# A four-mixer block reordered: fourth mixer first, input, conditioning and gate tiles beside its chain and beside attention

## Time and profile before

| | us |
|---|---|
| median of 3 runs | 2001.17 (2000.5 to 2010.23) |
| the profiled execution | 2002.8 |
| its span, first to last instruction | 2001.0 |
| mean matmul of the norm behind `out` (L711) starts at | 487.7 |
| TensorE busy, share of the span | 1791.4, 90% |
| VectorE busy | 955.8, 48% |
| ScalarE busy | 748.4, 37% |

### The profile page before, as it was taken

How to read it: one execution, slowest core, us unless ns; L and a number is a source line. 1 busy time by engine, 2 the same in 40 slices (tenths; PEclk the granted TensorE clock), 3 DMA queues, 4 the chain that set the end, 5 groups by cost and what they waited for, 6 DMA issues and landing times.

```text
span 2001.0 us, 33267 instructions
## 1 busy us (share of the span) xinstructions
PE 1791.4 (90%) x12858; PEld 1364.6 (68%) x12858; DVE 955.8 (48%) x1744; ACT 748.4 (37%) x1370; POOL 111.9 (6%) x170
## 2 busy tenths in 40 slices
PE   7987685997799999799999899999998799989997
PEld 7934344997544444377778588788875685779997
DVE  3552635665712211326444555434534454458684
ACT  4433212443222112242464443333325334555454
POOL 0200000004100000100000200000002000010000
PEclk9989796999799999989999899999998899989998
DMA  6887292556198899722100222322221230135552
GB/s 245 172 324 267 104 345 77 175 185 205 39 335 324 330 339 338 290 87 74 53 1 22 74 85 85 95 95 95 88 91 64 84 106 1 43 116 189 180 179 75
DMA packets 84994, 303.95 MB, mean 152 GB/s; under 512 B 10160, under 2 KB 12208, under 8 KB 84720
## 3 DMA queue, kind: packets, MB, share of 16 engines
q1 hardware_dynamic: 80784, 291.02, 42.2%
q0 software_dynamic: 2736, 7.35, 1.6%
q10 hardware_dynamic: 1328, 3.55, 0.4%
HBM read 347.74 MB, written 3.15 MB: 175 GB/s over the span
## 4 chain that ended last, share of the span: by engine, by line
PE 74%; DMA 12%; DVE 8%; ACT 4%; issue 2%; SPq 1%; POOL 0%; DVEq 0%; ACTq 0%; POOLq 0%
PE bank L766 49%; PE bank L711 16%; DMA ring<-wall 11%; PE bank L1193 3%; PE bank L790 2%; PE bank L1231 1%; PE bank L1206 1%; PE bank L1216 1%; ACT BIG L1481 1%; DVE w_lo L1823 1%; DVE BIG L2383 1%; ACT w_hi L1421 0%; ACT L1483 0%; ACT XC L1489 0%; PE bank L1253 0%
## 5 line engine op out<-in xcount | busy, mean ns | idle before, releaser
L766 PE MATMUL bank<-BIG_f32r,w_hi 128*128 128x256 f32 (+1 forms) x2208 | 554.0, 339 | 26.7 <-DVE BIG_f32r L1836 17.0
L1823 DVE TENSOR_TENSOR w_lo<-ring,w_hi 128x1024 fp32r<-128x1024 f32 x261 | 325.3, 1256 | 296.7 <-ACT w_hi L1421 295.5
L766 PEld LDWEIGHTS bank<-BIG_f32r,w_hi 128*128 128x128 f32 x2208 | 382.8, 192 | 75.7 <-issue 27.9
L766 PE MATMUL bank<-BIG_f32r,w_lo 128*128 128x256 f32 (+1 forms) x1136 | 385.8, 340 | 0.0
L1421 ACT ACTIVATE w_hi<-ring 128x1024 fp32r<-128x1024 f32 x261 | 272.5, 1053 | 223.6 <-PE bank L766 212.0
L766 PE MATMUL bank<-AR_f32r,w_hi 128*128 128x256 f32 (+1 forms) x1066 | 267.9, 330 | 16.7 <-issue 9.4
L766 PEld LDWEIGHTS bank<-BIG_f32r,w_lo 128*128 128x128 f32 x1136 | 216.8, 191 | 26.2 <-issue 0.2
L766 PEld LDWEIGHTS bank<-AR_f32r,w_hi 128*128 128x128 f32 x1066 | 185.2, 192 | 37.5 <-issue 9.9
L766 PE MATMUL bank<-AR_f32r,w_lo 128*128 128x256 f32 (+1 forms) x448 | 147.7, 330 | 0.0
L766 PE MATMUL bank<-XC_f32r,w_lo 128*128 128x256 f32 x424 | 122.4, 289 | 0.0
L766 PE MATMUL bank<-XC_f32r,w_hi 128*128 128x256 f32 x424 | 121.8, 287 | 0.0
(11 more groups left out here) (361 smaller groups left out, 2313.5 us busy)
## 6 DMA issues: line engine op xcount, KB each, us to landing
ring<-wall SPq DMA_DIRECT2D x547, 512.0 KB, 4.5
w_extra<-wall SPq DMA_DIRECT2D x96, 512.0 KB
BIG<-t_rows POOLq DMA_DIRECT2D x16, 128.0 KB, 14.4
AR<-na_rows POOLq DMA_DIRECT2D x32, 64.0 KB, 7.2
con<-consts ACTq DMA_DIRECT2D x1, 1810.0 KB, 12.2
na_rows<-rpb_pad POOLq DMA_DIRECT2D x1, 1792.0 KB, 34.8
XC<-xin ACTq DMA_DIRECT2D x1, 1024.0 KB, 6.4
XC<-ctxin POOLq DMA_DIRECT2D x1, 1024.0 KB, 6.1
```

Source lines behind the costliest of these rows:

```text
L766: ins = nc.tensor.matmul(o, l, r, start=start and n == 0, stop=stop and n == 2, **kw)
L1823: V.tensor_tensor(w_lo[:, i % SPLIT_RING, :], ring[:, t % RING, :], w_hi[:, i % SPLIT_RING, :].bitcast(F32), ALU.subtract).then_inc(w_spli ...
```

## The change

Nothing is computed otherwise, but in another order and in other places.

- The stream is no longer laid out stage by stage. A table `BESIDE` names the points of the program at which input tiles, gate tiles and pairs are worked off, and the stream follows it. Split and whole tiles now alternate, so `feed` looks ahead over the whole tiles in between, as far as the ring (six) and three split tiles reach.
- Order: the low-rank inputs and mixer d's inputs (7 tiles), d's features, its families and chunks, with the other 18 input tiles and 21 pairs beside them; then index scores, d's norm, attention with 23 gate tiles and 16 pairs, of which the choice of keys now takes two rounds in each of the first four steps; then mixer c with 9 gate tiles and 9 pairs; then eight branch tiles and eight out tiles in turns.
- Gates are copied out of PSUM as they come, all kept (8 x 1024 columns), and pass the sigmoid later, 1024 columns at once.
- `iw` has no tile of its own any more (8 columns inside `small`, transposed by a matmul): 169 tiles in place of 170.
- `out` is summed over k outermost into four banks that are all finished at the end; before, one result after another was finished.
- d's shift is done for each of the seven inputs as it arrives, where one 128 x 1792 and seven 128 x 256 operations were done at once.
- The 29 modulation operations run inside the expert loop, behind expert 2.

```diff
+BESIDE = {
+    "lora": ins_("small", "dr0", "dr1", "dk0"),
+    "kk": ins_("dk1", "dv0", "dv1"),
+    "feat": ins_("iq0", "iq1", "ik", "ckv") + ada_(2),
+    "split": ins_("bq0", "bq1") + ada_(2),
+    "Z1": ins_("cq") + ada_(1),
+    "D4": ada_(1),
+    "Z2": ins_("ck") + ada_(1),
+    "Z3": ins_("cv0"),
+    "Pm": ins_("cg0") + ada_(1),
+    "P2t": ins_("cg1", "aq0"),
+    "Y1": ins_("aq1") + ada_(1),
+    "T": ins_("ak0"),
+    "chain": ins_("ak1", "av0"),
+}
+for _c in range(NCH):
+    for _w in ("X", "U", "Yc"):
+        BESIDE[f"{_w}{_c}"] = ada_(1)
+BESIDE["var"] = gates_(7, 0, 1)
+BESIDE["std"] = ada_(2) + gates_(7, 2, 3)
+for _t in range(8):
+    BESIDE[f"att{_t}"] = ada_(2 if _t < 5 else 1) + gates_(6 - _t // 2, 2 * (_t % 2), 2 * (_t % 2) + 1)
+for _t in range(8, 11):
+    BESIDE[f"att{_t}"] = ada_(1) + gates_(2, _t - 8)
+BESIDE["c0"] = gates_(2, 3) + ada_(1)
+BESIDE["c1"] = gates_(1, 0, 1) + ada_(2)
+BESIDE["c2"] = gates_(1, 2) + ada_(1)
+BESIDE["c3"] = gates_(1, 3) + ada_(1)
+BESIDE["c4"] = gates_(0, 0, 1) + ada_(2)
+BESIDE["c5"] = gates_(0, 2, 3) + ada_(2)
...
+    def split_until(t):
+
+        if t >= moe0:
+            return split_at[min(t + SPLIT_RING, run_end(t + 1)) - 1] + 1
+        end = split_at[t]
+        while end < split_at[t] + SPLIT_RING and split_order[end] < min(t + RING, moe0):
+            end += 1
+        return end
...
+            for m in range(KC + 1):
+                if m < KC:
+                    for half in range(2):
+                        b = open_(("br", m, half))
+                        w = tile("branch", m)
...
+                if m:
+                    k = m - 1
+                    pe.wait_ge(sem("merged_split"), k + 1)
+                    w = tile("out", k)
+                    for o in range(KC):
+                        split_product(out_banks[o // 2][:, (o % 2) * S:(o % 2 + 1) * S], w, o, mg_hi[:, k, :],
...
+                    if st == "att1":
+                        beside(f"att{t}")
+                        if t < 4:
+                            choose(2 * t)
+                            choose(2 * t + 1)
+                        if t == 3:
+                            select()
...
+            in_unit("small")
+            in_unit("dr0")
+            in_unit("dr1")
+            act.wait_ge(sem("d_shifted"), 1)
...
+            dve.wait_ge(sem("params_in"), 16)
+            dve.wait_ge(sem("consts_in"), 16)
+            shifted(0)
...
+                if n == 2:
+                    modulation()
```

More of the change, by code:

```diff
@@ new lines, with early_stream @@
+BESIDE["c4"] = gates_(0, 0, 1) + ada_(2)
+BESIDE["c5"] = gates_(0, 2, 3) + ada_(2)
+R_W, R_A, R_G, R_C = 0, 32, 64, 96
+def early_stream():
+    items, pair = [], 0
+    for work in BESIDE.values():
+        for w in work:
+            if w[0] == "in":
+                items += [("in", IN_BLOCKS.index(n)) for n in (w[1], IN_PAIRS.get(w[1])) if n]
+            elif w[0] == "gate":
+                items.append(("gate", 4 * w[1] + w[2]))
+            else:
+                items += [("ada", 2 * pair), ("ada", 2 * pair + 1)]
+                pair += 1
+    for m in range(KC + 1):
+        if m < KC:
+            items.append(("branch", m))
+        if m:
+            items.append(("out", m - 1))
+    return items
@@ L1067, in _ @@
             family("Kt", pair(tok(DD["Kh"]), eye))
+            b = open_("bonus")
+            pe.wait_ge(sem("d_bonus_in"), 1)
+            mm(b, c_("blockones"), bn.rearrange("p a b -> p (a b)"), done="bonus")
+            beside("split")
             pe.wait_ge(sem("d_split"), 5)
@@ new lines, in _ @@
+            b = open_("ymean")
+            for c in range(NCH):
+                for p in range(2):
+                    evacuated(pe, ("Yc", c, p))
+            mm(b, c_("blockones"), yT.rearrange("p a b -> p (a b)"), done="ymean")
+            beside("var")
+            b = open_("yvar")
+            pe.wait_ge(sem("d_ysq"), 1)
+            mm(b, c_("blockones"), DD["t"].rearrange("p a b -> p (a b)"), done="yvar")
+            index_scores(1)
+            beside("std")
+            pe.wait_ge(sem("bias1"), 16 * 16)
@@ L1644, in _ @@
[L1644 to L1652 removed]
+            beside("c4")
@@ L1659, in _ @@
-            act.wait_ge(sem("merged"), KC)
-            tell(f(mg_hi[:, KC - 1, :], mergedT[:, KC - 1, :], ACT.Copy), "merged_high")
-            for m in range(KC):
-                feed("out", m)
+                    if m < KC:
+                        feed("branch", m)
+                    feed("out", m - 1)
             layer_norm("a")
@@ L2043, in _, with beside @@
-            step(ins, "ys_ready")
-            r_, k_, v_ = dS[:, 1:3, :], dS[:, 3:5, :], dS[:, 5:7, :]
-            evacuated(dve, "dw")
-            evacuated(dve, "da")
-            evacuated(dve, "dg")
-            for m in range(2):
-                ins = V.tensor_scalar(DD["kk"][:, m, :], k_[:, m, :], p_("d_k_k")[:, m:m + 1], None, ALU.mult)
-            step(ins, "d_kk")
+                    feed_to(k + 1)
+            def beside(point):
+                for work_ in BESIDE[point]:
+                    if work_[0] == "in":
+                        feed_in(work_[1])
+                    elif work_[0] == "gate":
+                        feed("gate", 4 * work_[1] + work_[2])
@@ L2110, in _ @@
                     evacuated(dve, (fam, p))
+            beside("chain")
             for c in range(NCH):
@@ L2162, in _ @@
+            step(V.reciprocal(c_sq, c_sq))
+            step(V.tensor_tensor(c_o, c_o, c_sq, ALU.mult))
+            for m in range(2):
+                ins = V.scalar_tensor_tensor(ysT[:, 2, m, :], c_o[:, m, :], p_("c_norm_gain")[:, m:m + 1],
+                                             F["cg"][:, m, :], ALU.mult, ALU.mult)
+            step(ins, "c_out")
+            ys_low(3, 3)
+            beside("c5")
+            ys_low(2, 4)
             b = bank(dve, "mods")
```

933 lines of the change are left out of this document (516 added, 417 removed).

## The result

Measured together, the changed kernel took 1980.57 us (median of 4, 1976.11 to 1985.88), the kernel before 2003.71 (median of 4): ratio 0.988, 95% interval 0.985 to 0.991. It is faster by 23 us. I forecast 1939 us, a saving of 64: right in direction, but 42 us too optimistic, with a saving little more than a third of the forecast's. The time lies inside the wide range (1893 to 1988) and outside the forecast's own (1915 to 1965).

What follows compares the result with a forecast made beforehand. Waiting left by the hand-written order was taken to decide, not TensorE's floor (348 us) or the ring's (254). Eight steps summed to 424.0 against 487.7, saving 63.7, hence 1939 us; own range 1915 to 1965, 8 in 10 from 1893 to 1988.

Steps and rivals of the forecast that it cites:

- step 1: From the start to d's features: 62.8 us, with eleven blocks of 32.6 us and three waits on top.
- the price of choice: Choice of keys inside attention's first four steps: 1.6 us a step, plus 2 us for the selected bias, 8.4 us.
- step 8: First norm: GpSimd's adds no longer run beside blocks, last add to mean matmul costs 4.5 us more, to 424.0.
- step 2: d's families and blocks: 79.7 us, to 142.5; 18.2 to the first squaring, then 61.5.
- step 3: Four chunks with twelve pairs beside them: 32 us, to 174.5; the pairs' 6 us lie in TensorE's gaps.
- step 4: Index scores and d's norm: 30 us, to 204.5, with four gate blocks of 11.5 and two waits.
- step 5: Attention: 109 us, to 313.5; the loop takes 25.6 us for two steps, with a gate tile landing behind four tiles.
- step 6: Mixer c: 50 us, to 363.5; nine gates 25.8, nine pairs 4.5, c's own 8, waits about 9.
- Steps 7 and 8: Branch and out in turns, 56 us at 6.1 for each of eight, then the norm's added 4.5, to 424.0.
- A: Rival, whole new order: the waits vanish as engines run ahead, 48 us less, 1891 us; chance 0.16.
- B: Rival, at 25 wait points: the clock falls, 1.55 us extra each, 39 us in all, 1978 us; chance 0.17.
- C: Rival, VectorE's queue: conversions waiting for tiles block it, 3.5 us at 25 points, 87 us, 2026 us; chance 0.09.

Runs made afterwards that it cites:

- e6: Changed kernel with all eight rounds of choice and the selected bias ahead of attention again, on VectorE; 1987.51 us.
- e8: Changed kernel with the first norm's sum made by seven TensorE matmuls instead of six GpSimd adds, seven VectorE routing operations moved behind the norm; 1977.09 us.
- e9: Changed kernel with the sixteen bias1 transfers held until the mean of d's result is read and na_rows until the merge; 1992.04 us.
- e1: Changed kernel with the one transfer na_rows issued right after the constants landed, instead of behind the bias1 transfers; 1978.89 us.
- e4: Changed kernel with conversions ahead ending at the next whole tile, from the gate tiles of d's norm to the branch; 2003.72 us.
- e5: Changed kernel with conversions ahead ending at the next whole tile, from d's norm's gate tiles only to gate (2, 1) of attention's tenth step; 1983.05 us.
- e11: Changed kernel with late bias1 and na_rows, the first norm's mean on TensorE, and pair and gate alternating in attention only; 1971.13 us.
- e15: Changed kernel with five of attention's pairs moved among the later families; 1971.64 us.
- e16: Changed kernel with five of attention's pairs among the later families, na_rows early and the norm's mean on TensorE; 1957.95 us, ratio to before 0.977.
- e3: Changed kernel with pair and gate tiles alternating in attention and in places of mixer c; 1973.25 us.
- e7: Changed kernel with the sigmoid taken when a gate is copied out of its bank, instead of later; 1981.62 us.
- e2: e1 with the bias rows t5 also computed ahead of the chain, so the sixteen bias1 transfers are issued earlier; 1987.82 us.
- e12: Changed kernel with five of attention's thirteen pairs moved in front of the features; 1975.1 us.
- e13: Changed kernel with eight pairs moved in front of the features, five left in attention; 1974.89 us.
- e14: e12 with na_rows early and the first norm's mean on TensorE; 1968.19 us.

## Why the prediction was right and wrong

**What held.** Blocks beside the chains keep the clock up and save time; step 1 (62.1 for 62.8); the price of choice (e6, 7.0 us for 8.4); step 8's adds (e8); the loop of branch and out, bound by TensorE, 265 matmuls in 32.05 us.

**The step that failed** is "Four pairs took 1.92 us, so 0.5 us a pair on TensorE". It is a term of the sum that was mis-sized: 0.96 us, and 0.26 for the picking, which the sum left out. Over 48 pairs that is 0.74 x 48 = 35 us of TensorE work, in a sum that came out 35.6 us too small. That the two numbers agree is chance. By the stages below the pairs can account for 20 us at most: 2.9 in step 2, 3.3 in step 3, 1.5 in step 4, 5.9 in step 5 and 6.7 in step 6. The largest miss, 16.2 us in step 2, is mostly other work that the sum priced too low. What fell on the path is seen stage by stage:

- *Step 2*, 61.5 us forecast from the first squaring on. In e9, where the transfers are away, the 71.1 us are 36.8 for twelve blocks (3.07 each between small work, 2.90 in the long run of blocks; forecast 34.4), 29.4 for everything else on TensorE (forecast 19.8), and 4.9 in which it was idle (forecast 7.3). In the 29.4, families took 1.04 to 1.08 us each and not 0.86, a price that the forecast gave without a row: 3 us more. Matmuls at the low clock were some 4 us, pairs and picking 2.9 (the forecast took six pairs, the table has five there), the rest small. The waits that I worried about were smaller than I said, and the work larger. GpSimd's transfers, which the forecast didn't name, added 4.6 us, nearly all of it `na_rows` (e1), and the part up to the first squaring 2.
- *Step 5* had the mechanism of its loop right: the next gate tile is issued when this step's pairs were read and lands behind four others. Forecast were 25.6 us for two steps, the chain took 28.3. So attention came out only 6 us longer than forecast. What no line of the forecast says is what hangs on the number of tiles: with five pairs fewer the gate tile lands in half the time, and 23 of the 97 us went, of which the work of these pairs on TensorE is 6. That the six slots fix the place of the gate tile in its row is read from the issues; no run changed their number.
- *Step 6*: nine pairs and pickings at 0.74 us too little are 6.7 of the 11 us; two ring waits on the chain, of 4.1 and 4.9 us, were the 9 us allowed. The rest stays unassigned.
- *Step 4*, 3.8 us over: by size, two pairs 1.5, four blocks 0.8, and a first block at the low clock (4.61 us) 1.5. *Step 3*, 3.3 over, holds twelve pairs, priced 8.9 us too low; the ring hides most of that. *Steps 7 and 8* came 3.9 us shorter: an eighth took 5.8 us and not 6.1.
- *Slips*: the 1.6 us by which the profiled execution lies above the median were named and not taken off (with them and the 3.8 us the sum gives 1941), the least time is 1863 by its own terms and not 1868, and the clock of 0.59 to 0.75 between 101 and 341 us holds for the chains alone; attention ran at 1.00 and the families at 0.96.

**The rivals.** A (waits vanish) didn't come. B had its price right: behind a long wait a block took 4.6 to 4.7 us for 3.07, 1.6 us where I said 1.55. But the chain behind the features has five such blocks (4.1 to 5.1 us) and not 25, 7.8 us in all, and some small matmuls beside them: the 24 behind the wait of 9.6 us in attention took 5.25 us, 3.75 by the earlier trace rows. The Trainium skill ("TensorE: Matmul & The Clock Gate", HAM oscillation) has the engine fall back to 1.2 GHz in each round of a loop that waits for a transfer. In attention the trace agrees behind TensorE's three longest idle times (5.4, 4.1 and 9.6 us); behind those of 1.1 to 1.3 us the clock stayed, and over the whole of attention it was 0.89.

C came by its own sign and not by its size. VectorE stood before `w_lo` 3.6 us a time in attention (47.4 in 13), over the 2.5 us that I had named. Yet without looking ahead attention is only 8 to 9 us shorter (e4, e5), the forecast's loop had a landing in it already, and looking ahead earns far more in mixer c. That the time landed on B's 1978 is a coincidence of sizes: most of the miss is work that was priced too low.

**Open.** In e1, e9, e11, e15 and e16 mixer c took 3.0 to 4.5 us more than its 63.2, with its program unchanged. The traces show where. In each of them one or two gate blocks ahead of the reciprocal ran at the low clock, 4.4 to 5.5 us for 3.1, and so it was in e3, e5 and e7. In the changed kernel and in e2, e6, e8, e12, e13 and e14, with mixer c at 61.9 to 64.8 us, none of these did. The same two blocks on the chain of the changed kernel and on that of e16:

```profile
356.35 3.11 PE bank L891 x24
...
368.70 3.11 PE bank L891 x24
```

```profile
340.76 4.60 PE bank L894 x24
...
355.23 4.60 PE bank L894 x24
```

That is rival B's mechanism, with 3.0 of the 4.0 us of e16. What tips the clock there no run says; that it is the phase in which mixer c meets the ring is a guess. Of the difference between e16 and e14 (23 us and 12 under the changed kernel), 7 lie in the families: the early `na_rows` took 7.1 us off them in e16 and 0.4 in e14. Why isn't settled.

## What to carry to other kernels

Count the records of one known unit (a pair, a block) in the trace before using its time: a call may leave more than one. When transfers and a chain share a loop, compare the tiles of one round with the number of slots as well as with the rate, and look at which place in a row of issues the tile has that the chain waits for. Here the step from six tiles to four, with six slots, brought it from fifth to first and was worth 23 us; fewer tiles than that gained little more. Work that only fills gaps is not free where the ring is full: a pair of 0.96 us cost 2.4 to 3.7 us there, and 4.7 where it took the last slots. And a stretch counted from one engine's landmark can hide what another engine did ahead of it: take the marks of the engine that has the work.

## What the runs showed of the hardware

Transfers of GpSimd that took 34% of the DMA engines doubled the ring's landing, 11.1 us in place of 5.7 in the same stretch without them, and cost the stretch 4.6 us. A tile of 512 KB that was issued first of its row in attention landed in 3.3 to 4.0 us, one that was issued fifth in 6.9 to 8.0. The sixteen loads of the bias cost about 1 us in the middle of the families (e1 against e9), 7 at their beginning (e2 against e1) and 9 behind the chunks (e9). These are differences of single executions; like ones differ by up to 3 us in the families. The four matmuls of a pair, each on 32 columns of the array, overlap: 16 records passed in 1.92 us, though the mean busy time of one in such a group is given as 608 to 692 ns. So the price of such work is read from the start and end of the group, not from count times mean.
